# A decoder layer in one kernel: x transposed once, raw, its transpose kept in DRAM for the residual, and the first norm applied after the transpose

## The reference, cut to what matters

```
def _layer(x, c, conv_prev, C0, n0, m0, w_ada, b_ada, g1n, g2n, w_in, ...):
    mod = (silu(c) @ w_ada + b_ada)[:, None, :]
    sh1, sc1, gt1, sh2, sc2, gt2 = split(mod, 6)
    h = _rmsnorm(x, g1n) * (1 + sc1) + sh1      # x / sqrt(mean(x*x) + EPS) * g1n
    mix, new_conv, C1, n1, m1 = _mixer(h, ...)  # h @ w_in, gates, conv, mLSTM, @ w_out
    x = x + gt1 * mix
    h = _rmsnorm(x, g2n) * (1 + sc2) + sh2
    x = x + gt2 * (square(relu(h @ w_up)) @ w_down)
```

## Time and profile before

| | |
|---|---|
| median of 3 runs | 1810.56 us |
| the runs | 1809.63 to 1813.29 us |
| span of the profiled execution | 1804.3 us |
| median less span | 6.26 us |
| TensorE busy in that span | 1775.4 us |
| VectorE busy | 759.9 us |
| ScalarE busy | 489.3 us |
| read from and written to DRAM | 120.86 MB and 17.80 MB |

### The profile page before, as it was taken

The page is one execution under the profiler, slowest core; times in us unless marked ns, Lnnn a source line. Parts: engine busy times, 40 slices in busy tenths (PEclk is TensorE's granted clock), DMA queues, the critical chain, the costliest instruction groups (busy, mean ns, idle before and its releaser), DMA issues.

```text
span 1804.3 us, 26783 instructions
## 1 busy us (share of the span) xinstructions
PE 1775.4 (98%) x10976; PEld 1713.8 (95%) x10976; DVE 759.9 (42%) x1445; ACT 489.3 (27%) x832; POOL 12.3 (1%) x25
## 2 busy tenths in 40 slices
PE   8999999999999999999999989999999999999997
PEld 3899999999999999999999989999999999999997
DVE  3644324444544545333353564343333333433345
ACT  5443333223333233211232341212121121212122
POOL 0000000000000000000000010000000000000000
PEclk9999999999999999999999989999999999999999
DMA  9444544322331232211132111111111111111112
GB/s 310 141 138 156 176 130 131 83 60 69 88 97 54 63 98 58 58 47 46 49 88 79 47 36 47 48 48 46 46 37 45 46 46 46 46 46 46 47 47 97
DMA packets 192677, 139.34 MB, mean 77 GB/s; under 512 B 15323, under 2 KB 176007, under 8 KB 192630
## 3 DMA queue, kind: packets, MB, share of 16 engines
q1 hardware_dynamic: 185910, 130.01, 24.4%
q10 hardware_dynamic: 6720, 8.67, 1.4%
HBM read 120.86 MB, written 17.80 MB: 77 GB/s over the span
## 4 chain that ended last, share of the span: by engine, by line
PE 95%; DVE 2%; DMA 1%; issue 1%; ACT 1%; SPq 0%; DVEq 0%; ACTq 0%
PE PB L916 85%; PE M L844 3%; PE M L969 1%; PE M L860 1%; PE M L1044 1%; DMA araw<-in_w_ada 1%; PE M L1050 1%; PE M L1036 1%; PE M L1038 1%; DVE XL L1223 1%; PE M L908 0%; PE M L1014 0%; DVE R L1709 0%; ACT A L532 0%; PE M L1061 0%
## 5 line engine op out<-in xcount | busy, mean ns | idle before, releaser
L916 PE MATMUL PB<-XH,whi 128*128 128x352 f32 x2496 | 811.3, 325 | 4.1 <-DVE XL L1223 2.1
L916 PE MATMUL PB<-XH,wlo 128*128 128x352 f32 x2496 | 801.5, 321 | 0.0
L916 PE MATMUL PB<-XL,whi 128*128 128x352 f32 x2496 | 801.3, 321 | 0.0
L916 PEld LDWEIGHTS PB<-XH,whi 128*128 128x128 f32 x2496 | 469.0, 188 | 11.3 <-issue 6.9
L916 PEld LDWEIGHTS PB<-XL,whi 128*128 128x128 f32 x2496 | 470.2, 188 | 0.7
L916 PEld LDWEIGHTS PB<-XH,wlo 128*128 128x128 f32 x2496 | 468.7, 188 | 0.0
L550 ACT ACTIVATE whi<-raw 128x1024 fp32r<-128x1024 f32 x134 | 141.3, 1054 | 407.4 <-PE PB L916 404.3
L916 PE MATMUL PB<-AH,whi 128*128 128x352 f32 x720 | 233.1, 324 | 0.2 <-issue 0.2
L916 PE MATMUL PB<-AL,whi 128*128 128x352 f32 x720 | 232.5, 323 | 0.0
L916 PE MATMUL PB<-AH,wlo 128*128 128x352 f32 x720 | 232.1, 322 | 0.0
L1228 DVE TENSOR_TENSOR wlo<-raw,whi 128x1024 fp32r<-128x1024 f32 x134 | 163.7, 1222 | 118.0 <-ACT whi L550 117.1
(11 more groups left out here) (297 smaller groups left out, 1199.4 us busy)
## 6 DMA issues: line engine op xcount, KB each, us to landing
raw<-in_w_in SPq DMA_DIRECT2D x64, 512.0 KB, 4.8
araw<-in_w_ada SPq DMA_DIRECT2D x48, 512.0 KB, 5.3
raw<-in_w_up SPq DMA_DIRECT2D x32, 512.0 KB, 4.0
raw<-in_w_down SPq DMA_DIRECT2D x32, 512.0 KB, 3.4
zp_d<-zr ACTq DMA_DIRECT2D x16, 512.0 KB, 2.7
Z<-zp_d SPq DMA_DIRECT2D x8, 1024.0 KB, 5.8
xin<-in_x_prompt SPq DMA_DIRECT2D x8, 512.0 KB, 7.0
CU<-in_state_C SPq DMA_DIRECT2D x8, 512.0 KB, 3.8
```

Of the source, the lines that this page charges most:

```text
L916: ins = pe.matmul(PB[:, bank, 0:BLK], w[:, w0:w0 + P], x[:, k, a0:a1], start=(k == 0 and j == 0), stop=(k == n_k - 1 and j == 2))
```

## The change

xin is transposed as it comes, without the norm. A stays raw, and the whole of it is stored once to a DRAM tensor `xt_d`, from which phase 4 loads `xT` (three slots) already transposed. 1/rms is applied to the transposed x: VectorE's `xdiag(g)` writes a diagonal of 1/rms into the first 128 columns of each block in `xin`, once that block is transposed. Nine matmuls of `ones` with these diagonals spread the values over all partitions, and ScalarE copies them to `RX`. `hf(k)` writes A * S1 * RX to a buffer `HN`, `h_hi(k)` adds the shift as the bias of its activation, and `h_lo(k)` adds it again as it subtracts. The samples get a buffer of their own, `HX`.

```diff
 # SyncE
         sp.wait_ge(s["xt_done"], 9)
+        sp.wait_ge(s["rx_done"], 1)
+        sp.dma_start(xt_d.rearrange("k p n -> p k n"), A[:]).then_inc(s["xt_out"], 16)
         atile(0, 0, 0, 2048)
         atile(1, 1, 1, 2048)
...
-        def load_xs(n, slot):
-            sp.dma_start(xs[:, slot, 0:8, :], x_p[:, :, bass.ds(n * P, P)]).then_inc(xs_in[slot], 16)
-            sp.dma_start(xs[0:NS, slot, 8, :], x_s[:, bass.ds(n * P, P)]).then_inc(xs_in[slot], 16)
+        def load_xt(n):
+            sp.dma_start(xT[:, n % 3, :], xt_d[n]).then_inc(xt_in[n % 3], 16)
...
+        sp.wait_ge(s["xt_out"], 16)
+        for n in range(3):
+            load_xt(n)
+        for n in range(KT - 2):
+            tile(T4_ + 2 + n, n % 2, w_out[:, :, P * n + 2 * P:P * n + 3 * P])
+            if n + 3 < KT:
+                sp.wait_ge(acc_free[2], P4_ + n + 1)
+                load_xt(n + 3)
 # ScalarE
         squares(2)
+        for b in range(6, 9):
+            xt_evac(b)
...
         def h_hi(k):
             act.wait_ge(s["hf_done"], k + 1)
-            act.activation(XH[:, k, :], A[:, k, :], ACT.Copy).then_inc(s["h_hi"], 1)
+            act.activation(XH[:, k, 0:TP], HN[:, k % 2, 0:TP], ACT.Identity, bias=MOD[:, k, 0:1]).then_inc(s["h_hi"], 1)
+
+        def hs_hi(i):
+            act.wait_ge(s["hx_done"], i + 1)
+            act.activation(XH[:, 4 * i:4 * i + 4, TP:T], HX[:, 4 * i:4 * i + 4, :], ACT.Copy).then_inc(s["hx_hi"], 1)
 
         hi(0, 0)
-        for b in range(6, 9):
-            xt_evac(b)
+        act.wait_ge(s["rx_mm"], 1)
+        act.activation(RX[:, 0:TP], PB[:, 0:2, :].rearrange("p a n -> p (a n)"), ACT.Copy)
+        act.activation(RX[:, TP:T], PB[:, 2, 0:NS], ACT.Copy).then_inc(s["rx_done"], 1)
         for k in range(KT):
+            if k % 4 == 0:
+                hs_hi(k // 4)
             h_hi(k)
...
 # phase 4
-                act.wait_ge(s["xtr_done"], n + 1)
-                if not (isinstance(i, int) and n == 0):
-                    act.wait_ge(acc_free[2], P4_ + n)
-                act.activation(xT[:, 0:TP], M[:, 0:2, :].rearrange("p a n -> p (a n)"), ACT.Copy)
-                act.activation(xT[:, TP:T], M[:, 2, 0:NS], ACT.Copy).then_inc(s["xtr_copy"], 1)
 # TensorE
         def xturn(b):
-            pe.wait_ge(s["xn_done"], b + 1)
+            pe.wait_ge(xr[b], 16)
...
         rowt0(2)
+        pe.wait_ge(s["pool_done"], POOL_STEPS)
+        pe.wait_ge(s["rx_diag"], 1)
+        pe.wait_ge(s["xt_free"], 8)
+        for b in range(9):
+            n = P if b < 8 else NS
+            ins = pe.matmul(PB[:, b // 4, P * (b % 4):P * (b % 4) + n], ones[0:n, :], xin[0:n, b, 0:n], start=True, stop=True)
+        ins.then_inc(s["rx_mm"], 1)
         ada0(3)
         rowt0(3)
...
 # phase 4
-                pe.wait_ge(xs_in[x], 32 * i + 32)
-                if isinstance(i, int) and n == 0:
-                    pe.wait_ge(s["fin1_copy"], 2)
-                else:
-                    pe.wait_ge(s["xtr_copy"], n)
-                for b in range(8):
-                    turn(M[:, b // 4, P * (b % 4):P * (b % 4) + P], xs[:, x, b, :])
-                turn(M[:, 2, 0:NS], xs[0:NS, x, 8, :]).then_inc(s["xtr_done"], 1)
 # VectorE
-        def xnorm(g):
+        def xdiag(g):
...
             for b in range(3 * g, 3 * g + 3):
                 n = P if b < 8 else NS
-                dve.tensor_scalar(xin[0:n, b, :], xin[0:n, b, :], rs[0:n, b:b + 1], None, ALU.mult).then_inc(s["xn_done"], 1)
+                dve.wait_ge(s["xt_done"], b + 1)
+                ins = dve.tensor_scalar(xin[0:n, b, 0:n], ident[0:n, 0:n], rs[0:n, b:b + 1], None, ALU.mult)
+            if g == 2:
+                ins.then_inc(s["rx_diag"], 1)
...
+            if k0 == 0:
+                dve.wait_ge(s["xt_free"], 9)
+                dve.wait_ge(s["rx_done"], 1)
+                link(dve.tensor_tensor(HX[:], HS, RX[:, TP:T].rearrange("p (o n) -> p o n", o=1).to_broadcast([P, KT, NS]), ALU.mult))
+            link(dve.tensor_tensor(hx[:, k0:k0 + 4], hx[:, k0:k0 + 4], bc(S1[:, k0:k0 + 4, 1:NB]), ALU.mult))
+            dve.tensor_tensor(hx[:, k0:k0 + 4], hx[:, k0:k0 + 4], bc(MOD[:, k0:k0 + 4, 1:NB]), ALU.add).then_inc(s["hx_done"], 1)
...
         def hf(k):
-            dve.tensor_scalar(A[:, k, 0:TP], A[:, k, 0:TP], S1[:, k, 0:1], MOD[:, k, 0:1], ALU.mult, ALU.add) \
-               .then_inc(s["hf_done"], 1)
+            if k >= 2:
+                dve.wait_ge(s["h_lo"], k - 1)
+            stt(HN[:, k % 2, 0:TP], A[:, k, 0:TP], S1[:, k, 0:1], RX[:, 0:TP], ALU.mult, ALU.mult).then_inc(s["hf_done"], 1)
 
         def h_lo(k):
+            if k % 4 == 0:
+                hs_lo(k // 4)
             dve.wait_ge(s["h_hi"], k + 1)
-            dve.tensor_tensor(XL[:, k, :], A[:, k, :], XH[:, k, :].bitcast(F32), ALU.subtract).then_inc(s["h_lo"], 1)
+            stt(XL[:, k, 0:TP], HN[:, k % 2, 0:TP], MOD[:, k, 0:1], XH[:, k, 0:TP].bitcast(F32), ALU.add, ALU.subtract) \
+                .then_inc(s["h_lo"], 1)
...
         h_lo(1)
+        hf(3)
         arow0(3)
-        hf(3)
         h_lo(2)
...
+        dve.wait_ge(s["xt_out"], 16)
         phase2(0)
...
-                dve.wait_ge(s["xtr_copy"], n + 1)
+                dve.wait_ge(xt_in[n % 3], 16 * (n // 3 + 1))
```

More of the change, by code:

```diff
@@ L147, in layer_kernel @@
     NB0, DL, MU = RMK[0:H], NBr[0:H], TH[0:H]
+    RX = xin[:, 4:6, :].rearrange("p a n -> p (a n)")[:, 0:T]
+    HN = zr
+    HS = A[:, :, TP:T]
     RR = sb("RR", [H, T], scope=gates)
@@ L230, in layer_kernel @@
     araw_in = [s["araw_in0"], s["araw_in1"]]
-    xs_in = [s["xs_in0"], s["xs_in1"]]
+    xt_in = [s[f"xt_in{i}"] for i in range(3)]
     y_out = [s["y_out0"], s["y_out1"]]
@@ L517, in squares @@
                 act.wait_ge(xr[b], 16)
-                own.link(act.activation(junk[0:n, :], xin[0:n, b, :], ACT.Square, accum_out=ss[0:n, b:b + 1]))
+                own.link(act.activation(XL[0:n, 0, 0:D], xin[0:n, b, :], ACT.Square, accum_out=ss[0:n, b:b + 1]))
             if g < 2:
@@ L1283, in modulate_samples, with hs_lo @@
                      PC[:, G1R + k0:G1R + k0 + 4].rearrange("p (x o) -> p x o", o=1).to_broadcast([P, 4, NB]), ALU.add, ALU.mult))
[L1284 to L1286 removed]
+            if k0 == 0:
[4 more added lines that the diff above has]
+            dve.tensor_tensor(hx[:, k0:k0 + 4], hx[:, k0:k0 + 4], bc(MOD[:, k0:k0 + 4, 1:NB]), ALU.add).then_inc(s["hx_done"], 1)
+        def hs_lo(i):
+            dve.wait_ge(s["hx_hi"], i + 1)
+            dve.tensor_tensor(XL[:, 4 * i:4 * i + 4, TP:T], HX[:, 4 * i:4 * i + 4, :], XH[:, 4 * i:4 * i + 4, TP:T].bitcast(F32), ALU.subtract)
         def hf(k):
[L1289 to L1290 removed]
+            if k >= 2:
+                dve.wait_ge(s["h_lo"], k - 1)
+            stt(HN[:, k % 2, 0:TP], A[:, k, 0:TP], S1[:, k, 0:1], RX[:, 0:TP], ALU.mult, ALU.mult).then_inc(s["hf_done"], 1)
         def h_lo(k):
+            if k % 4 == 0:
+                hs_lo(k // 4)
             dve.wait_ge(s["h_hi"], k + 1)
[L1294 to L1296 removed]
+            stt(XL[:, k, 0:TP], HN[:, k % 2, 0:TP], MOD[:, k, 0:1], XH[:, k, 0:TP].bitcast(F32), ALU.add, ALU.subtract) \
+                .then_inc(s["h_lo"], 1)
+        xdiag(0)
         arow0(0)
@@ L1304, in _ @@
         mod0(0)
-        xnorm(1)
+        xdiag(1)
         dve.wait_ge(s["small_in"], 16 * 4)
@@ L1317, in _ @@
         mod0(1)
-        xnorm(2)
+        xdiag(2)
         arow0(2)
@@ L1638, in residual @@
             if b < 2:
-                stt(an[:, a0:a1], PB[:, b, 0:BLK], gt[:, 0:1], xT[:, a0:a1], ALU.mult, ALU.add).then_inc(acc_free[b], 1)
+                stt(an[:, a0:a1], PB[:, b, 0:BLK], gt[:, 0:1], xT[:, n % 3, a0:a1], ALU.mult, ALU.add).then_inc(acc_free[b], 1)
             else:
-                stt(an[:, a0:TP], PB[:, b, 0:LP], gt[:, 0:1], xT[:, a0:TP], ALU.mult, ALU.add)
+                stt(an[:, a0:TP], PB[:, b, 0:LP], gt[:, 0:1], xT[:, n % 3, a0:TP], ALU.mult, ALU.add)
                 link(dve.tensor_tensor(an[:, TP:T].rearrange("p (b t) -> p b t", t=ST),
@@ L1644, in residual @@
                                        gt[:, 1:NB].rearrange("p (b o) -> p b o", o=1).to_broadcast([P, SB, ST]), ALU.mult))
-                dve.tensor_tensor(an[:, TP:T], an[:, TP:T], xT[:, TP:T], ALU.add).then_inc(acc_free[b], 1)
+                dve.tensor_tensor(an[:, TP:T], an[:, TP:T], xT[:, n % 3, TP:T], ALU.add).then_inc(acc_free[b], 1)
         def scaled(n, a0, a1):
@@ L1674, in phase4 @@
                 assert own.n == PER4, own.n
-        with dve.Fori(0, KT // 2 - 1) as i:
+        for i in range(KT // 2):
             phase4(i)
-        phase4(KT // 2 - 1)
         own.turn(base4, KT - 1, PER4)
```

28 lines of the change are left out of this document (8 added, 20 removed).

## The result

The changed kernel's median is 1810.82 us (20 runs, 1808.90 to 1814.94), that of the kernel before in the same sitting 1808.06 us (20 runs, 1805.96 to 1813.29). The ratio is 1.0017 [1.0011, 1.0023]: slower by 2.8 us, just under the 0.2% that the prediction took as the bound of what can be told; the interval excludes 1. The spans are 1808.3 us after and 1804.3 us before, +4.0, where the sum said +4.1. Both spans are of one execution each; over the 20 runs of the changed kernel the span goes from 1807.1 to 1813.2 us. Most of that error is in the time that stands for the kernel before, and is taken up with the terms.

The account below looks back on a forecast made before the run. TensorE, busy 98% of the span, was taken to bound the kernel. Start +9.3, clock +2.2 and phase 4 -7.35 gave +4.1: span 1808.4, plus 6.26 to the median, 1814.7 us, 0.23% slower; range 1811.0 to 1818.5.

Parts of the forecast that it names:

- the sum: Whole span: +9.3 us at the start, +2.2 for the clock, -7.35 in phase 4, making +4.1.
- the rival in which the clock holds: Ahead of the first product, 4.0 us of idleness doesn't lower the clock: +1.9, 1812.5 us; chance 0.20.
- Waits behind the diagonals: Start's three rounds: row turns wait for VectorE's copy behind the diagonals, 1.09, 1.76 and 1.18 us, together 4.0.
- Two thirds TensorE's queue, one third the order: First product 9.3 us later: two thirds TensorE's queue, one third arow0(3) put behind hf(3).
- Rigid afterwards: After the gate copies everything moves rigidly; nothing later gives time back, since TensorE is full.
- The rx matmuls: Start: nine matmuls spreading 1/rms cost TensorE 2.1 us, bounds 1.1 and 2.7.
- The clock: TensorE's clock falls once, behind 4.0 us of idleness ahead of the first product: 2.2 us.
- this rival: Clock falls earlier too, behind the second round's 1.76 us wait: 2.2 to 2.7 us more, 1817.1; chance 0.14.
- Phase 4: Output product: seven of eight transpose groups come off TensorE at 1.05 us each, gain 7.35, bounds 7.3 and 8.4.
- the hidden first group: Phase 4's first transpose group gains nothing, since the product waits for VectorE's first low half anyway.
- The store: Start, SP's queue: 4.33 MB hidden, landing by 71, about 4 us slack; late-store rival 1820 and more, chance 0.08.
- The start bound by loads: Rival: start's rounds wait for w_ada anyway, so 6.1 us of waits and matmuls vanish: 1808.6; chance 0.10.

Follow-up runs that it names:

- e11: The changed kernel run once more, unchanged: 1812.01 us, ratio 1.0025 to the kernel before.
- e5: The changed kernel with 28 extra, unread TensorE matmuls ahead of the start's four row turns: 1806.19 us, ratio 0.9991 to the kernel before.
- e2: The changed kernel with VectorE's conditioning-row copy ahead of the three diagonals in each of three rounds: 1804.82 us, ratio 0.9984 to the kernel before.
- e3: The changed kernel with arow0(3) put back ahead of hf(3) on VectorE: 1808.22 us, ratio 1.0005 to the kernel before.
- e6: The changed kernel with the 4.33 MB store issued twice, the second copy unread: 1818.84 us, ratio 1.0062 to the kernel before.
- e9: The changed kernel's start, store included, with phase 4 of the kernel before: 1817.55 us, ratio 1.0060 to the kernel before.
- e10: e9 without the store and the wait for it: 1819.72 us, ratio 1.0061 to the kernel before.
- e4: The changed kernel with the order changes of e2 and e3 together: 1804.53 us, ratio 0.9979 to the kernel before.
- e1: The kernel before with only phase 4's transposes and copies dropped, residual loaded from untransposed rows: 1799.64 us, ratio 0.9958 to the kernel before.
- e7: The changed kernel with both orders of e4 and the store issued as soon as A is whole: 1804.46 us, ratio 0.9977 to the kernel before.
- e8: e7 with arow0(3) one step earlier, directly behind hf(2): 1803.04 us, ratio 0.9970 to the kernel before.
- e12: e8 with extra unread matmuls in three TensorE waits (fourth row turn, phase 4, second norm): 1808.21 us, ratio 1.0003 to the kernel before.

## Why the prediction was right, by its steps

**The kind of result was right**: slower, by the start's lateness less phase 4's transposes, with the clock on top. The span's difference was +4.0 and, in e11, +3.8, against +4.1. Where terms missed, they missed against one another.

That these two numbers agree to 0.1 us is luck. The spans of the changed kernel's 20 runs lie between 1807.1 and 1813.2 us, those of the kernel before in three later sittings between 1803.9 and 1810.7. The medians differ by 2.8 us (2.0 to 4.2 by the interval of the ratio), which lies about midway between the forecast's 4.1 and the 1.9 of the rival in which the clock holds. The time alone doesn't decide between them; the traces and e5 do.

| term | predicted | changed kernel | e11 |
|---|---|---|---|
| third rowt0 later by | 4.0 | 5.58, 1.69 of it clock | 3.75 |
| rx matmuls, to the next start | 2.1 | 3.56 | 2.31 |
| start of ada0(3) later by | 6.1 | 9.16 | 6.09 |
| idle ahead of the fourth rowt0 | 4.0 | 3.35 | 3.67 |
| first gate matmul | 60.9 | 63.71 | 60.76 |
| gate copies later by | 11.5 | 13.60 | 11.44 |
| first output product later by | 11.5 | 12.96 | 11.29 |
| phase 4 | -7.35 | -8.90 | -7.65 |

**Waits behind the diagonals.** Right in place and size. In e11 the second rowt0 starts at 35.71 against 33.04, 2.67 for the first two rounds (predicted 1.09 + 1.76), and the third at 46.88 against 43.13, 1.08 more (predicted 1.18). e2 took them away.

**Two thirds TensorE's queue, one third the order.** Right for the queue: 6.09 of 9.16 us in e11. The order of arow0(3) and hf(3) is less than a third: e3 cut the last wait from 3.67 (e11) or 3.35 us to 1.46, some 2 us. The rest of that wait is VectorE's chain from the rx matmuls on. e2 took 3.8 us off the rounds.

**Rigid afterwards.** Nearly: between the gate copies and the first output product 0.64 us came back (e11: 0.15), where the prediction said none.

**The rx matmuls.** Taken at 2.1, they are 2.29 us at full clock (e2) and 3.56 at the lower one. The choice of the row of the second norm was right. The 4.4 us by the factor of the Trainium skill ("TensorE: Matmul & The Clock Gate", Terms) is not what these rows show: eight transposes of 128 columns take 0.93 us to the next group's start (30.82 to 31.75 in the changed kernel), 0.12 each, and an extra matmul of 128 columns took 0.24 in e5, a factor of 2.1.

**The clock.** This term was mis-sized: 2.2 us in the sum, 4.6 by e5. The prediction let the clock fall once, ahead of the first product, for 2.2 us. In e11 it did just that in the start, for 2.3 us (11.44 less 9.16). In the first profile it fell three times, and the two more falls cost 1.7 and 1.3 us. The argument against this rival, that 1.76 us of wait is no longer than the 1.84 us ahead of phase 4, was not good enough: a wait of one length lowered the clock in one execution and not in the next. Over all profiles with that wait of 1.65 us the clock fell in the next product in three (changed kernel, e3, e6) and held in three (e9, e10, e11). The kernel before had an answer too. The fall at 1036.6, which the prediction set beside 4.0 us of idleness, comes 0.2 us after a wait of only 1.69 us:

```profile
1036.41 0.47 PE L1108 MATMUL M<-ones,SQA 128*128 128x1 f32 x2 [1.69 <-ACT SQ L745]
```

So a wait shorter than 1.76 us already stood ahead of a fall in that trace. What a case shows once is a chance, and I had read it as a rule.

**Phase 4.** Mis-sized in two ways. A group's 1.05 us is the time of its transposes; taken from start to start, with the change of queue from products to transposes and back, seven groups cost 8.90 us, 1.27 each. The chain of waits shows durations, and the start of the neighbours would have given the rest. Against that stands the hidden first group. The prediction costed it at nothing, since the product waits for the low half anyway; but without it the idleness is 2.89 us instead of 1.84, and the clock, which may fall there with either wait, is worth 1.3 to 1.6 us:

| kernel | wait ahead, us | clock behind it | first output product to second norm, us |
|---|---|---|---|
| before, e9 | 1.84 | held | 94.70, 94.70 |
| e10 | 1.84 | fell | 96.28 |
| after, e3, e4, e6 | 2.89 | held | 85.80, 85.79, 85.77, 85.80 |
| e1, e2, e5, e7, e8, e11 | 2.89 | fell | 87.20, 87.24, 87.13, 87.24, 87.37, 87.05 |
| e12 | filled | held | 85.64 |

**The store.** Right: hidden (e10), landed in 13.7 us, and with little slack behind it. It was issued at 59.99 and not at 56.5, so it landed near 73.7 and not by 71. The slack I put at about 4 us. A second store made ScalarE's first cast wait 9.87 us; with 12.8 us for that store, that leaves 3 us, an estimate. In e3 and e9, with one store, the first cast waited 0.40 and 0.25 us for its load. That its rate in the start would be that of the stores in the earlier trace rows was right: 12.8 and 2 for landing against 13.7.

**The start bound by loads.** Wrong as a rival: TensorE waited for w_ada once, 1.54 us, as in the kernel before (1.4), and the added waits and matmuls of the start didn't vanish in that one. The waits of ScalarE that I followed in e4 and e7 stand in the kernel before as well.

**The time itself.** 1814.7 was the sum plus 6.26 us, the distance of the first three runs' median to one span. In the later profiles the profiled execution took 1.7 us more than its span (1810.01 against 1808.3 in the changed kernel). Runs of the kernel before took 1.7 to 2.9 us more than theirs; which holds for its profiled execution isn't on record, and I take 1.7. The rest, 4.6 us, is then the spread between executions: 1804.3 + 1.7 = 1806.0 lies at the lower end of before's 20 runs, the median of the three in their upper half. With 20 runs before's median is 1808.06; 1808.4 + 1.7 would have been 1810.1.

**What stays open.** Why the clock falls behind one wait of 1.65 or 1.84 us and holds behind another of 2.89 is not settled, nor is what makes it fall in the second norm in every profile; no run here moves one thing alone that would tell it. How often it falls I know only from these few profiles: ahead of phase 4, behind 2.89 us, in e1, e2, e5, e7, e8 and e11, and not in after, e3, e4 and e6.

## What to carry to other kernels

An instruction added to an engine that is far from busy is free only if nothing that the full engine waits for stands behind it: here three diagonals of 0.2 us, placed ahead of a copy instead of behind it, cost 3.8 us and the clock's share on top. When work is taken out of a wait, or a short wait is put among matmuls, cost the clock as well, as a chance with a price (here 1.3 to 2.3 us each time), and try the order of the queue before anything else. Take what leaves a full queue from start to start, not by its duration.

## What the runs showed of the hardware that I had not expected

- The same program at the same place, behind the same wait of 1.65 us, ran its next product at full clock in one execution and partly at the lower one in another (7.04 against 8.73 us). The Trainium skill, "TensorE: Matmul & The Clock Gate", Part 1: The HAM clock gate, says of a kernel's start that the same kernel shows different numbers of slow matmuls from run to run. These two profiles show the like in mid-kernel.
- Behind the last wait of the start the clock fell where that wait was 2.34 us (e4, e7) or 3.06 to 3.67 us (after, e2, e6, e9, e10, e11), and held where it was 0.77 (before, e1), 1.14 (e8) or 1.46 us (e3). Behind TensorE's wait for w_ada at 16 us it fell where that wait was 2.01 to 2.15 us (e8, e10, e12) and held in the eleven profiles where it was 0.96 to 1.99. At these two places the length of the wait sorts the falls. It doesn't in the rounds (1.65 us, three of six fell) or ahead of phase 4 (1.84 us, one of three; 2.89 us, six of ten).
- A store of 4.33 MB from SBUF to DRAM beside other transfers landed in 12.5 to 13.8 us, 315 to 345 GB/s, about the 339 GB/s of a stretch of stores alone.
